# Router products streamed in four column groups, one inverse root by ScalarE's square root, and expert ranks from bf16 constants, in a hybrid decoder block

## The reference

```python
def moe(h, w_router, b_router, w_gate_up, b_gate_up, w_down, b_down):
    logits = (h2 @ w_router + b_router).astype(jnp.float32)     # (256, 32)
    top_v, top_i = lax.top_k(logits, TOP_K)
    gates = jax.nn.softmax(top_v, axis=-1)
    ...
    # tokens sorted by expert, each expert's rows through
    # (up + 1) * gate * sigmoid(1.702 * gate), then w_down
    # and added back with their gates
x = x + moe(rmsnorm(x, norm_moe_w), ...)
return rmsnorm(x, norm_final_w)
```

## Time and profile before

| | us |
|---|---|
| median of three runs (1199.46 to 1199.58) | 1199.49 |
| the profiled execution | 1199.3 |
| its span | 1197.5 |
| PE busy | 1149.4 (96%) |
| VectorE (DVE) busy | 377.9 (32%) |
| ScalarE (ACT) busy | 171.6 (14%) |
| GpSimd (POOL) busy | 18.5 (2%) |
| DMA, mean over the span | 371 GB/s |

### The profile page before, as it was taken

One profiled execution on the slowest core, in us unless ns is written; L12 is line 12 of the kernel. 1 busy time (PEld: TensorE's weight loads), 2 busy tenths in 40 slices (PEclk: granted clock), 3 DMA queues, 4 the chain that ended last, 5 costly groups with the idle time before them and its releaser, 6 DMA issues.

```text
span 1197.5 us, 17800 instructions
## 1 busy us (share of the span) xinstructions
PE 1149.4 (96%) x7104; PEld 577.9 (48%) x7105; DVE 377.9 (32%) x885; ACT 171.6 (14%) x343; POOL 18.5 (2%) x57
## 2 busy tenths in 40 slices
PE   9999999999999999999999999999999999999997
PEld 5989869956434434334333434333333333333332
DVE  4788787646212221112221212112121111111112
ACT  4311321243101100000000100000000000000002
POOL 3000010000000000000000000000000000000000
PEclk9999999999999999999999999999999999999999
DMA  9953300997999999999999999999999999999995
GB/s 303 375 184 115 109 9 17 405 342 304 409 426 427 438 429 429 434 428 432 435 429 431 436 427 432 432 430 432 433 430 432 433 430 431 431 433 426 424 425 227
DMA packets 42850, 444.85 MB, mean 371 GB/s; under 512 B 6308, under 2 KB 6772, under 8 KB 26040
## 3 DMA queue, kind: packets, MB, share of 16 engines
q1 hardware_dynamic: 41912, 441.63, 88.3%
q0 software_dynamic: 480, 1.85, 0.6%
q10 hardware_dynamic: 416, 0.79, 0.2%
HBM read 443.20 MB, written 1.05 MB: 371 GB/s over the span
## 4 chain that ended last, share of the span: by engine, by line
PE 68%; DMA 30%; ACT 0%; SPq 0%; DVE 0%; issue 0%; DVEq 0%; ACTq 0%
DMA ring<-in_w_gate_up 30%; PE bank L1101 23%; PE bank L1092 13%; PE bank L725 6%; PE bank L721 4%; PE bank L1124 4%; PE bank L1139 3%; PE bank L704 2%; PE bank L713 2%; PE bank L769 2%; PE bank L807 1%; PE bank L1031 1%; PE bank L1212 1%; PE bank L1115 1%; PE bank L1203 1%; PE bank L944 1%
## 5 line engine op out<-in xcount | busy, mean ns | idle before, releaser
L1101 PE MATMUL bank<-ring,region 128*64 128x512 f32 x2048 | 463.4, 608 | 36.6 <-DMA ring<-in_w_gate_up 36.6
L1101 PEld LDWEIGHTS bank<-ring,region 128*64 128x64 f32 x2048 | 147.0, 140 | 334.5 <-issue 270.4
L1092 PE MATMUL bank<-ring,region 128*64 128x512 f32 x1024 | 226.8, 595 | 0.2 <-ACT region L1332 0.2
L2143 DVE TENSOR_SCALAR region<-bank 128x512 f32<-128x512 f32 x32 | 22.1, 692 | 573.7 <-PE bank L1101 573.7
L1092 PEld LDWEIGHTS bank<-ring,region 128*64 128x64 f32 x1024 | 71.1, 137 | 130.0 <-issue 127.2
L1332 ACT ACTIVATE region<-bank 128x256 f32<-128x256 f32 (+1 forms) x134 | 55.6, 440 | 371.0 <-PE bank L1092 251.0
L1332 ACT ACTIVATE bank<-region 128x512 f32<-128x512 f32 x32 | 19.2, 601 | 452.9 <-DVE region L2143 452.9
L725 PE MATMUL bank<-ring 128*128 128x256 f32 x336 | 73.8, 380 | 0.0
L725 PEld LDWEIGHTS bank<-ring 128*128 128x128 f32 x336 | 63.3, 190 | 9.3 <-issue 0.5
L1124 PE MATMUL bank<-region 64*128 64x512 f32 x264 | 65.6, 615 | 0.1
L1139 PEld LDWEIGHTS bank<-region,r_levels 128*128 128x128 bf16 x1584 | 63.1, 117 | 1.8 <-issue 1.6
(11 more groups left out here) (286 smaller groups left out, 785.4 us busy)
## 6 DMA issues: line engine op xcount, KB each, us to landing
ring<-in_w_gate_up SPq DMA_DIRECT2D x48, 4096.0 KB, 30.2
ring<-in_w_down SPq DMA_DIRECT2D x24, 4096.0 KB, 36.9
ring<-in_w_gate_up SPq DMA_DIRECT2D x26, 2048.0 KB, 14.8
ring<-in_w_down SPq DMA_DIRECT2D x10, 2048.0 KB, 13.5
ring<-in_w_in SPq DMA_DIRECT2D x6, 2048.0 KB, 17.2
ring<-in_w_gate_up SPq DMA_DIRECT2D x11, 1024.0 KB, 34.3
ring<-in_w_xkv SPq DMA_DIRECT2D x4, 2048.0 KB, 10.0
ring<-in_w_down SPq DMA_DIRECT2D x7, 1024.0 KB, 8.9
```

The costliest lines, as they stand in the source:

```text
L1092: last = pe.matmul(bk[half * ROWS:(half + 1) * ROWS, :], lhs, w[:, half * 512:(half + 1) * 512], start=start, stop=stop, skip_group_check= ...
L1101: last = pe.matmul(rows, lhs, columns[:, half], start=start, stop=stop, skip_group_check=True)
```

## The change

1. **Router products.** The sides are swapped: 32 columns of the router's weights are stationary, and 128 tokens of `h2T` are streamed. Feature tile k goes to column group k mod 4, so that four products of 32 columns stand side by side in the array and their sums land in four groups of 32 partitions. All eight feature tiles of tile 0 go this way, and the first four of tile 1; these four are moved up, between the halves of `xo11`. ACT copies the 128x128 result to SBUF (`logit_parts`), and one product with a new 0/1 matrix `group_sum` adds the four groups and turns the result back to tokens by experts (`sum_of_groups`). For tile 1 the last four feature tiles are added to it in the old form. GpSimd makes `group_sum` with five more operations.
2. **Inverse root of tile 1.** ACT takes the square root of the mean square; DVE does the reciprocal and one Newton step in place of `newton_steps`. The square-root table is loaded (`preload_act_table_set`) after ACT's second `logit_parts` copy.
3. **Ranks.** `chosen`, the strict matrix and the ones are bf16, and the order of the products changes: `keep_warm` before the bias is gone, one dummy product (two instructions) stands between the products of tile 0 and the wait for tile 1's `chosen`, and both counts follow that wait. The ranks lie in `bank_d` in place of `bank_a`.
4. Some semaphores are merged (`x_squared` with `mem_squared`, `z_exp` with `z_ln`), with the counts moved accordingly.

```diff
+            def logits_in_groups(bk, tiles, stop):
+                for k in tiles:
+                    g = k % (P // E)
+                    last = pe.matmul(bk[g * E:(g + 1) * E, 0:P], w_router[:, k, :], h2T[:, k, :], start=(k < P // E), stop=stop or k >= P // E)
+                return last
+            def sum_of_groups(bk, t, stop):
+                pe.wait_ge(sem["parts_kept"], t + 1)
+                return pe.matmul(bk[:, P:P + E], logit_parts, group_sum, start=True, stop=stop)
             bk = begin("router0")
-            for k in range(KT):
-                await_rows({0: ["eT00"], 4: ["eT01"]}, k)
-                last = pe.matmul(bk[:, 0:E], h2T[:, k, :], w_router[:, k, :], start=(k == 0), stop=(k == KT - 1))
-            end(last)
+            wait_taken(pe, "eT00")
+            logits_in_groups(bk, range(0, KT // 2), False)
+            wait_taken(pe, "eT01")
+            logits_in_groups(bk, range(KT // 2, KT), False).then_inc(sem["router_parts"], 1)
             flip_rows("eT", 1, 0, "xo")
+            end(sum_of_groups(bk, 0, True), "router0")
...
                         last.then_inc(sem["eT_part"], 1)
+                        routed = begin("router1")
+                        wait_taken(pe, "eT10")
+                        logits_in_groups(routed, range(0, KT // 2), True).then_inc(sem["router_parts"], 1)
...
-            routed = begin("router1")
-            wait_taken(pe, "eT10")
-            for k in range(KT // 2):
-                route(k)
+            sum_of_groups(routed, 1, False)
             wait_taken(pe, "xo11")
...
-            pe.wait_ge(sem["iota_ready"], 1)
-            keep_warm()
...
-            wait_taken(pe, "router1")
-            pe.matmul(rank_psum[:, 0:E], rank_strict, chosen[:, 0, :], start=True, stop=True)
+            wait_taken(pe, "xo11a")
+            pe.matmul(rank_psum[:, 0:E], strict, chosen[:, 0, :], start=True, stop=True)
             pe.matmul(rank_psum[:, E:2 * E], rank_ones, chosen[:, 0, :], start=True, stop=False)
+            keep_warm(1)
+            pe.wait_ge(sem["chosen_ready"], NT)
+            pe.matmul(rank_psum[:, E:2 * E], strict, chosen[:, 1, :], start=False, stop=True)
             pe.matmul(count_psum, chosen[:, 0, :], rank_ones[:, 0:1], start=True, stop=False)
-            pe.wait_ge(sem["chosen_ready"], NT)
-            pe.matmul(rank_psum[:, E:2 * E], rank_strict, chosen[:, 1, :], start=False, stop=True)
             pe.matmul(count_psum, chosen[:, 1, :], rank_ones[:, 0:1], start=False, stop=True).then_inc(sem["rank_psum"], 1)
...
# ScalarE
+            act.wait_ge(sem["router_parts"], 1)
+            fn(logit_parts, bank_of("router0")[:, 0:P], ACT.Copy).then_inc(sem["parts_kept"], 1)
             half_squared(1, 0)
...
             fn(h2T[:, 4:6, :], tiles("eT11", P)[:, 0:2, :], ACT.Copy).then_inc(sem["h2T_part"], 1)
+            act.wait_ge(sem["router_parts"], 2)
+            fn(logit_parts, bank_of("router1")[:, 0:P], ACT.Copy).then_inc(sem["parts_kept"], 1)
+            nc.scalar.preload_act_table_set("sqrt_and_others")
             cut(3, 1)
             cut(3, 2)
             seed(1, 0, "eT10")
             wait_taken(act, "xo11")
             squared(x_res[:, 1, HALF + QUARTER:D], sq_quarter[:, 1:2], bank_u)
+            fn(roots[:, 0:1], sq_quarter[:, 1:2], ACT.Sqrt, bias=sq_partial).then_inc(sem["roots_ready"], 1)
...
# VectorE
             link(v.tensor_tensor(mean, sq_partial, sq_quarter[:, 1:2], ALU.add))
-            link(newton_steps(rstd[:, 7:8], mean))
+            root, slope, square = rstd[:, 7:8], newton[:, 2, 0:1], newton[:, 1, 0:1]
+            link(v.tensor_scalar(slope, mean, -0.5, None, ALU.mult))
+            dve.wait_ge(sem["roots_ready"], 1)
+            link(v.reciprocal(root, roots[:, 0:1]))
+            link(v.scalar_tensor_tensor(square, root, root, slope, ALU.mult, ALU.mult))
+            link(v.scalar_tensor_tensor(root, square, 1.5, root, ALU.add, ALU.mult))
             choose(1)
```

More of the change, by code:

```diff
@@ L308, in build @@
         sq_quarter, sq_partial = stat[:, 4:6], stat[:, 6:7]
-        logits, chosen, gate_ex = (small[:, c:c + NT * E].rearrange("p (t e) -> p t e", t=NT) for c in range(0, 192, 64))
+        logits, gate_ex = (small[:, c:c + NT * E].rearrange("p (t e) -> p t e", t=NT) for c in (0, 128))
+        chosen = small[:, 64:64 + NT * E // 2].bitcast(BF16).rearrange("p (t e) -> p t e", t=NT)
         left = small[:, 192:192 + NT * E].rearrange("p (t e) -> p t e", t=NT)
@@ L620, in _ @@
             link(pool.memset(rank_ones, 1.0))
-            pool.affine_select(out=rank_strict, in_=rank_ones, compare_op=ALU.is_gt, fill=0.0, base=0,
+            link(pool.memset(group_sum, 0.0))
+            for first in range(0, P, E):
+                link(pool.affine_select(out=group_sum, in_=group_sum, compare_op=ALU.not_equal, fill=1.0, base=-first, pattern=[[-1, E]],
+                                        channel_multiplier=1))
+            pool.affine_select(out=strict, in_=rank_ones, compare_op=ALU.is_gt, fill=0.0, base=0, pattern=[[1, P]], channel_multiplier=-1)
+            pool.affine_select(out=rank_strict, in_=all_ones, compare_op=ALU.is_gt, fill=0.0, base=0,
                                pattern=[[1, P]], channel_multiplier=-1).then_inc(sem["rank_consts"], 1)
@@ L1068, in route @@
             def route(k):
-                return pe.matmul(routed[:, 0:E], h2T[:, k, :], w_router[:, k, :], start=(k == 0), stop=(k == KT - 1))
-            routed = begin("router1")
-            wait_taken(pe, "eT10")
-            for k in range(KT // 2):
-                route(k)
+                return pe.matmul(routed[:, P:P + E], h2T[:, k, :], w_router[:, k, :], start=False, stop=(k == KT - 1))
+            sum_of_groups(routed, 1, False)
             wait_taken(pe, "xo11")
@@ L1105, in bias_of, with keep_warm @@
                 pair_of_inner(bk, one_hot, b_gu[:, c0:c0 + D], True, False)
-            def keep_warm():
-                for n in range(KEEP_WARM):
+            def keep_warm(products=KEEP_WARM):
+                for n in range(products):
                     pe.matmul(bank_g[:, 0:T], ident[:, :], iota, start=True, stop=True)
@@ L1374, in _ @@
             act.wait_ge(sem["z_abs"], 1)
-            fn(ez, ez, ACT.Exp).then_inc(sem["z_exp"], 1)
-            act.wait_ge(sem["z_exp"], 1)
+            fn(ez, ez, ACT.Exp).then_inc(sem["z_ln"], 1)
+            act.wait_ge(sem["z_ln"], 1)
             fn(l_z, ez, ACT.Ln, bias=1.0).then_inc(sem["z_ln"], 1)
@@ L1728, in _ @@
             for t in range(NT):
-                row_rms(t, 2, sem["mem_squared"]).then_inc(sem["mem_rms"], 1)
+                row_rms(t, 2, sem["rows_squared"], before=NT).then_inc(sem["mem_rms"], 1)
             dve.wait_ge(sem["lb_in"], 16)
@@ L2075, in choose @@
                 wait_full(dve, job)
[L2076 removed]
+                taken(v.scalar_tensor_tensor(logits[:, t, :], bank_of(job)[:, P:P + E], rstd[:, 6 + t:7 + t], b_router, ALU.mult,
                                              ALU.add), job)
```

32 lines of the change are left out of this document (17 added, 15 removed).

## The result

The changed kernel takes 1202.03 us (median of 20 runs, 1200.05 to 1203.57) beside 1199.53 for the kernel before (20 runs on the same chip): ratio 1.0018, 95% interval 1.0012 to 1.0023. By the ratio it is slower by about 2.2 us (1.4 to 2.8; the medians differ by 2.5), and it lies outside the predicted range of 1198.4 to 1201.3. The profiled execution took 1202.5 us with a span of 1200.8, 3.3 more than before.

The account below looks back on a forecast made before the run. The weight stream was taken to set the end, released by the router stage. Gains of 0.7 + 0.3 us, 1.25 lost, 0.5 reserve and 0.3 cheaper products made the stage 0.15 us later: 1199.6 us, range 1198.4 to 1201.3.

Parts of the forecast that it names:

- the clock rival: Router stage: PE's holes halve the clock for some 3.4 us, costing at most 1.7 us: 1201.3 us; chance 0.13.
- the holes: PE idle in the router stage: 284.7 to 285.95, 286.65 to 287.75 and 289.2 to 289.5 us.
- The path: Router stage to expert 0 to the issue of expert 2's first chunk at 300.44 us: shifts move the end one for one.
- the 1.0 us gained: PE up to xo11: 0.7 us from tile 0's grouped products and 0.3 us from tile 1's first half.
- the 1.25 us at the copy: ACT's copy of the last eT11 tiles starts at 287.3 instead of 286.04 us, behind the table load and square root.
- 0.5 and 0.3: End of the router stage: 0.5 us of reserve before PE uses chosen, 0.3 us back from bf16 rank products.
- ACT comes through sooner: Router stage: ACT's queue follows the earlier transposes; up to 1.8 us earlier, 1197.7 us, half taken, 1198.6; chance 0.25.
- The table loads stall longer: ACT in the router stage: each table switch holds it another 1.38 us, giving 1202.4 us; chance 0.04.
- The stage moves but the end does not: Weight stream: an earlier issue of the load list, at the 282 to 284 us hole, sets the end: 1199.4 us; chance 0.06.

Follow-up runs that it names:

- only_root: Kernel before plus only ACT's square root of tile 1 with its two table loads, dummy products kept: ratio 1.0031.
- fill_holes2: Changed kernel plus two dummy products on bank_d in each of PE's two holes: ratio 1.0002 to the kernel before.
- newton_fill: Changed kernel with newton_steps back on DVE, no added table loads, remaining holes filled with dummy products: ratio 0.9993 to the kernel before.
- root_fill: Kernel before plus only the square root and its table loads, with dummy products in PE's two waits: ratio 1.0014.
- only_ranks: Kernel before plus only the bf16 ranks in new order, dummies ahead of the bias removed, one ahead of the wait for chosen: ratio 1.0001.
- fill_first: Changed kernel with two dummy products in the first hole only, ahead of the wait for xo11: ratio 1.0008 to the kernel before.
- fill_second: Changed kernel with two dummy products in the second hole only, ahead of the wait for eT11: ratio 1.0006 to the kernel before.
- dve_hole: Kernel before plus a memset and four additions on a spare tile on DVE ahead of xo11's addition: ratio 1.0029.

## Why the prediction was wrong

**The step that failed is the clock rival**, in chance and in size. It had the right place, the holes at the last transposes and the last router products, and the right cause. Its case against itself was "no single hole here is as long as 2.63 us". It took one long wait in the expert phase as the measure for a place of a different kind, and length as what decides, though it had itself noted waits of the same length without a fall. Here PE's work between the waits is small, transposes and products of 32 columns, and 0.86 and 0.83 us were enough. The trace of before has one wait of 0.17 us in its stage, so nothing there gave the size of wait that the place bears. The forecast itself therefore stood at a clock of 1.00 through the stage, and put nothing into its sum for the clock. The dummy products that the change removes are not needed for the fall: only_root kept them all and fell. The size: one stretch of 3.4 us at 1.7 us at most, against 6.83 us measured, which costs 2.67 - 0.18 = 2.5 us here and 2.9 in only_root. Per microsecond at half the clock the price was right, at most a half; the length was twice what it had. The forecast of 1199.6 and 2.5 make 1202.1, where 1202.03 was measured. That they meet within 0.1 us is in part luck, since the change's executions lie 3.5 us apart and the ratio gives 2.2 us.

**The path held, and without the clock its end too.** With the waits filled the stage is 0.17 to 0.19 us longer, forecast 0.15. The line of the prediction that adds up the terms does not give 0.15 as it stands: the 1.0 us gained does not enter, since PE waits it away, and of the 1.25 us at the copy only 0.9 reach `choose(1)`, because before the change `newton_steps` held it until 0.36 us after the router's product (287.15 to 287.51). 0.9 less 0.5 and 0.3 is 0.1, or unrounded 289.75 - 289.61 = 0.14. Taking the 0.41 us off after's times:

- Grouped products of tile 0: 0.64 us (0.6 forecast), `xo11a` at 277.00 (277.04).
- Table load at 283.37 (283.4), an activation 0.01 us behind its end. The copy of the last `eT11` tiles at 287.14 (287.3), so 1.10 us late and not 1.25. The last router products at 287.55 (287.75).
- The holes: 0.86 us for 1.25, and 0.83 for 1.1. Behind them the errors nearly cancel: by fill_holes2, `choose(1)` starts at 288.29 (288.4), PE has `chosen` at 289.46 (289.5), and the three bf16 products take 0.26 us (0.2).
- Wrong without consequence: PE was to be 1.0 us ahead behind `xo11`. It was 0.6: before, PE was through the first four router products at 285.53, where the transposes start; now it could go on at 284.90 (the sum of the groups starts at 285.17 - 0.41, and in fill_holes2 the next product starts 0.14 behind it). The eight grouped products with the transposes take 0.66 us where the transposes alone took 0.22, so 0.44 for 0.3, and the `xo` products on either side got 0.08 and 0.10 us longer. The wait behind them hid it.

**ACT comes through sooner** (0.25): fell. ScalarE's queue did not follow PE: its copy of the first `eT11` tiles starts at 283.23 - 0.41 = 282.82 us, forecast 282.75. It priced a free table load at 1.8 us gained. No run has the square root without a load. The nearest, newton_fill, has neither and a filled stage, and gains 0.53 us where the ranks alone gain 0.60; its `choose(1)` starts 0.03 us behind the end of `newton_steps` on DVE, so that earlier router products bring nothing there. The lower end of the range, 1198.4 us, stood for the likely half of this rival; the lowest of the change's 20 executions is 1200.05 us.

**The table loads stall longer** (0.04): fell as a mechanism, though its 1202.4 us is nearly the time measured. The load at 283.78 us is followed at once, and so is root_fill's; one that held ScalarE for another 1.38 us would have left that gap. The Trainium skill, page "ScalarE: Activation LUTs", section "What ACT_TABLE_LOAD costs", gives 1283 ns for the load, and the trace agrees (1.28 us); it gives about 1380 ns of drain with it, and no run here shows that. A time that fits two rivals is told apart by their rows alone.

**The stage moves but the end does not** (0.06): fell, the issue and the span moved by 3.07 and 3.3 us.

## What to carry to other kernels

When a change takes work off TensorE or puts it behind another engine, list the waits that it leaves there together, with what is done between them, and price the clock for that stretch, not wait by wait. Neither a wait's length nor the sum of the waits is a safe measure, so test it: put a dummy product on a free bank into one of them, and look at the mean clock of many executions, since one profiled execution can miss the fall. A dummy product that ends within a wait costs nothing (the last transposes start at the same point in fill_holes2 and in the change), so taking it out gains nothing and may cost a clock stretch. And a table load ahead of the activations that the path waits for costs about its full 1.28 us: root_fill, which has four small VectorE operations in place of eight for it, is 1.31 us longer in the stage.

## What the runs showed of the hardware

- **Two short waits among small products brought the granted clock from 1.00 to 0.50 for 6.83 us.** With 0.86 and 0.83 us (after), and 0.45 and 0.83 (only_root), it fell; with 0.83 and 0.28 (fill_first), or 0.86 and 0.27 (fill_second), it stayed. It came back to 1.00 while PE was busy without a pause. The fall cost 2.5 to 2.9 us. The Trainium skill, page "TensorE: Matmul & The Clock Gate", section "A second HAM failure mode: psum-queue depth-cycling", reports of a bf16 kernel with products of 512 columns that brief idling between groups of products came often enough to make the clock swing between the two levels. These runs agree in that short waits can do it, here once in the stage.
- **The sum of the waits does not order the cases.** only_ranks has 0.17 and 0.56 us and a low mean clock in 8 of 11 executions, fill_second has 0.86 and 0.27 us and a low one in 1 of 10. What they differ in that matters stays open.
- **A wait of 1.15 us is harmless in one place and not in another.** Between products of 512 columns in the expert phase of the kernel before, eight waits of 1.10 to 1.36 us left the clock at 1.00; in the router stage of dve_hole one of 1.15 us brought it down for 13.65 us.
- **The length of the fall differs**: 3.41, 6.83 and 13.65 us. The longest followed one wait of 1.15 us and one of 0.17, shorter in sum than the change's two. What decides it stays open. It is not the program alone: dve_hole's executions differ among themselves, and in the trace of the kernel before the same wait of 2.63 us is followed by a fall eight times and by none twice.
- **A table load has no drain to be seen** on either side: 0.02 us from the activation ahead of it, 1.28 us, and 0.01 us to the next activation, in after and in root_fill.
